# A two-layer encoder trunk on one core: the expert stage rewritten in blocks of 32 slots, with a ring of nine weight units

## The reference

```
h = layer_norm(DN_ALPHA * h + mix, ln1_g[l], ln1_b[l])
g_idx = top-1 of softmax(h @ w_rg + b_rg)           # one group of 4
e_val, e_loc = top-2 of the 4 experts of that group
combine[token, expert] = softmax(e_val) * g_val
for e in range(16):
    out += combine[:, e:e+1] * ((silu(h @ w_gate[e]) * (h @ w_up[e])) @ w_down[e])
h = layer_norm(DN_ALPHA * h + ffn, ln2_g[l], ln2_b[l])
```

## Time and profile before

| | |
|---|---|
| median of 3 runs | 1976.12 us (1970.1 to 1976.12) |
| the profiled execution's own time | 1975.3 us |
| its span | 1973.2 us, so 2.1 us lie outside the span |
| PE busy | 1681.7 us |
| DVE, ACT, POOL busy | 609.8, 509.5, 87.2 us |
| DMA | 547.06 MB, mean 277 GB/s |
| PE's granted clock, mean | 0.956 of full speed |

### The profile page before, as it was taken

How to read it: one execution, slowest core, us unless ns; L and a number is a source line. 1 busy time by engine, 2 the same in 40 slices (tenths; PEclk the granted TensorE clock), 3 DMA queues, 4 the chain that set the end, 5 groups by cost and what they waited for, 6 DMA issues and landing times.

```text
span 1973.2 us, 22680 instructions
## 1 busy us (share of the span) xinstructions
PE 1681.7 (85%) x9061; PEld 1086.5 (55%) x9062; DVE 609.8 (31%) x714; ACT 509.5 (26%) x562; POOL 87.2 (4%) x39
## 2 busy tenths in 40 slices
PE   5899999968878788787869999999688777887885
PEld 5799899854322223232468999988433222222332
DVE  7745645542000000000386464564510000000005
ACT  4343444311111111111234543432111111111120
POOL 4100000003000000000040000000030000000000
PEclk9899999989999999999979999999799999999998
DMA  8354455650999999999514544558249999999961
GB/s 289 134 170 140 147 169 181 242 226 22 426 428 425 425 427 426 425 427 400 180 64 171 175 144 141 176 191 312 93 170 426 426 426 427 425 426 428 426 290 43
DMA packets 119302, 547.06 MB, mean 277 GB/s; under 512 B 19940, under 2 KB 23240, under 8 KB 84680
## 3 DMA queue, kind: packets, MB, share of 16 engines
q1 hardware_dynamic: 117600, 546.02, 69.6%
q10 hardware_dynamic: 1640, 0.13, 0.1%
HBM read 544.04 MB, written 2.10 MB: 277 GB/s over the span
## 4 chain that ended last, share of the span: by engine, by line
PE 55%; DMA 24%; PEldq 5%; DVE 5%; issue 5%; PEld 2%; ACT 2%; DVEq 1%; SPq 0%; ACTq 0%
DMA ring<-in_w_up_dram 24%; PE ps L705 20%; PE ps L843 9%; PE ps L900 6%; PEldq L681 5%; PE ps L702 4%; PE ps L917 4%; PE ps L881 3%; PE ps L954 3%; PEld ps L900 2%; DVE w_lo L964 1%; DVE hT_lo L964 1%; PE ps L945 1%; PE ps L667 1%; DVE arena L964 1%
## 5 line engine op out<-in xcount | busy, mean ns | idle before, releaser
L900 PE MATMUL ps<-ring,arena 128*64 128x512 f32 x2048 | 482.0, 625 | 99.0 <-DMA ring<-in_w_up_dram 75.5
L900 PEld LDWEIGHTS ps<-ring,arena 128*64 128x64 f32 x2048 | 175.5, 143 | 384.9 <-issue 384.9
L964 DVE TENSOR_TENSOR w_lo<-ring,w_hi 128x2048 fp32r<-128x2048 f32 x120 | 283.9, 2378 | 260.1 <-ACT w_hi L433 259.6
L705 PE MATMUL ps<-hT_hi,w_hi 128*128 128x256 f32 x1152 | 333.4, 289 | 25.1 <-DVE w_lo L964 24.6
L705 PE MATMUL ps<-hT_hi,w_lo 128*128 128x256 f32 x1152 | 330.0, 286 | 0.0
L705 PE MATMUL ps<-hT_lo,w_hi 128*128 128x256 f32 x1152 | 329.7, 286 | 0.0
L433 ACT ACTIVATE w_hi<-ring 128x2048 fp32r<-128x2048 f32 x120 | 228.0, 1914 | 250.0 <-PE ps L705 133.4
L964 DVE TENSOR_TENSOR arena<-arena,ps 128x256 f32<-128x256 f32 (+1 forms) x34 | 15.9, 468 | 793.4 <-ACT arena L630 793.2
L705 PEld LDWEIGHTS ps<-hT_hi,w_hi 128*128 128x128 f32 x1152 | 225.3, 196 | 28.7 <-issue 17.9
L917 PE MATMUL ps<-ring,arena 128*64 128x512 f32 x1024 | 226.8, 595 | 15.1 <-ACT arena L632 15.1
L705 PEld LDWEIGHTS ps<-hT_hi,w_lo 128*128 128x128 f32 x1152 | 225.3, 196 | 0.7 <-issue 0.5
(11 more groups left out here) (216 smaller groups left out, 1346.3 us busy)
## 6 DMA issues: line engine op xcount, KB each, us to landing
ring<-in_w_down_dram SPq DMA_DIRECT2D x64, 2048.0 KB, 18.3
ring<-in_w_gate_dram SPq DMA_DIRECT2D x64, 2048.0 KB, 16.3
ring<-in_w_up_dram SPq DMA_DIRECT2D x64, 2048.0 KB, 20.7
ring<-in_w_in_dram SPq DMA_DIRECT2D x88, 1024.0 KB, 4.8
ring<-in_w_out_dram SPq DMA_DIRECT2D x32, 1024.0 KB, 5.1
ring<-in_ln_g_dram SPq DMA_DIRECT2D x3, 1024.0 KB, 5.9
ring<-in_ln_b_dram SPq DMA_DIRECT2D x3, 1024.0 KB, 6.9
h<-in_x_dram SPq DMA_DIRECT2D x2, 1024.0 KB, 6.2
```

The lines of the kernel that those rows point to most:

```text
L705: last = eng.matmul(ps[:, b + o // 2, (o % 2) * T:(o % 2) * T + T], w_[:, o * P:o * P + P], x_[:, kk, :], start=opens and o % 2 == 0, stop ...
L900: last = eng.matmul(ps[64 * c:64 * c + BLK, 0, :], xe[:, k, :], ring[:, 0:2, k * 512 + c * 256:k * 512 + c * 256 + 256], start=(k == 0), s ...
L964: return eng.tensor_tensor(o, a, b, op)
```

## The change

Blocks have 32 slots. No rows are sorted ahead: in every block PE gathers the rows of the *next* block from h (`gather`, 8 products of 512 columns in four column groups; h is now the streamed operand, and its elements are read 64 bytes apart), turns them (`turn_rows`, 4 transposes), and scatters the outputs of the block *before* (`scatter`, 8 products whose contraction is 32 slots, in four row groups and four PSUM banks). The second four of these wait for DVE to have added the first four's banks into acc (`add_block`). Gate and up take 64 products of 256 columns in four column groups, down takes 16 of 512 in four. DVE marks the next block's slots (`mark`) and builds the scatter's matrix (`place`). The gather, transposes and scatter over all slots are gone, and so are yT, xgT and ySort. h must have its gain and bias before the gather, so that `affine(gb)` moves up to right after the transposes of the router, half of its first product on DVE. The ring has nine units of 16 KB of each partition (2.1 MB) instead of six; two units are released at a time. The expert loop is written out 16 times, with a loop only for the blocks beyond an expert's last. Before that, x is loaded in four pieces, the first `normalize` no longer waits for the parameters' transpose, the softplus stands between splits 17 and 18 (slab three of the trunk), and `affine(gb_in)` waits until PE has used nine quarters.

```diff
-BLK = 64
+BLK = 32
 KB = 256
-SLOTS = 3
...
+    SLOTS = 9
+    PER_E = 6
...
+        SLOT_KIB = (64, 80, 112, 0, 16, 128, 32, 48, 96)
...
+                    eng.wait_ge(units_used, PER_E * E * l - 2)
+                for n in range(2):
                     load_quarter(l, n)
+                if l:
+                    eng.wait_ge(units_used, PER_E * E * l)
+                for n in range(2, UNITS):
+                    load_quarter(l, n)
...
+                for u in range(PER_E * E):
+                    e, i = u // PER_E, u % PER_E
+                    if u >= SLOTS:
+                        eng.wait_ge(units_used, PER_E * E * l + u - SLOTS + 1)
+                    elif u == 2:
+                        eng.wait_ge(w_used.sem, w_used.at(l, 4 * N_IN))
+                    elif u == 3:
+                        eng.wait_ge(w_used.sem, w_used.at(l, NQ - 4))
+                    elif u == 4:
+                        eng.wait_ge(w_used.sem, w_used.at(l, NQ - 2))
+                    elif u == 6:
+                        eng.wait_ge(w_used.sem, w_used.at(l, NQ))
+                    if i < 4:
+                        for m, w in enumerate((w_gate, w_up)):
+                            src = w[l, e].rearrange("(p k) n -> p k n", k=KD)
+                            eng.dma_start(unit_gu(u)[:, m], src[:, 4 * i:4 * i + 4, :]).then_inc(unit_loaded[u % SLOTS], 16)
...
+                eng.wait_ge(w_used.sem, w_used.at(l, 9))
                 affine(gb_in)
                 eng.wait_ge(gb1_loaded.sem, gb1_loaded.at(l, 32))
-                eng.wait_ge(gath_done.sem, gath_done.at(l, KD))
-                affine(gb)
+                eng.wait_ge(xnT_done, (2 * l + 2) * 8)
+                eng.tensor_tensor(h[:, 1, :], h[:, 1, :], gb[:, 0, :], ALU.mult)
+                eng.drain()
+                eng.tensor_tensor(h[:, 1, :], h[:, 1, :], gb[:, 1, :], ALU.add).then_inc(h_ready, 1)
+                eng.wait_ge(aff_mul.sem, aff_mul.at(l, 1))
+                eng.tensor_tensor(h[:, 0, :], h[:, 0, :], gb[:, 1, :], ALU.add).then_inc(h_ready, 1)
...
+                for t in range(NT):
+                    last = eng.activation(acc[:, t, :], h[:, t, :], ACT.Copy)
+                last.then_inc(acc_ready.sem, 1)
+                with eng.Fori(0, nb) as j:
+                    g = g0 + j
+                    eng.wait_ge(gu_done, g + 1)
+                    eng.activation(sgate, ps[:, 0, 0:P], ACT.Silu).then_inc(sg_ready, 1)
+                    copy_of(xrow_done, g + l + 2, xrow, 3, xrow_ready)
+                    copy_of(hmT_done, g + 1, hmT, 1, hmT_ready)
+                    copy_of(xT_done, g + l + 2, xe, 3, xe_ready)
+                    copy_of(y_done, g + 1, yraw, 2, y_ready)
...
+                def gather(count):
+                    eng.wait_ge(hot_ready, count)
                     for t in range(NT):
...
+                        for c in range(4):
+                            r0 = BLK * c
+                            last = eng.matmul(ps[r0:r0 + BLK, 3, :], hot[:, t, :],
+                                              h[:, t, :].rearrange("a (p k) -> a k p", k=KD)[:, 4 * c:4 * c + 4, :],
+                                              start=(t == 0), stop=(t == NT - 1), tile_position=(0, r0))
+                    last.then_inc(xrow_done, 1)
+                def turn_rows(count):
+                    eng.wait_ge(xrow_ready, count)
+                    for q in range(4):
+                        last = eng.transpose(ps[:, 3, q * P:q * P + P], xrow[:, q * P:q * P + P], ident[:])
+                    last.then_inc(xT_done, 1)
...
+                def scatter(g):
+                    eng.wait_ge(place_ready, g + l + 1)
+                    eng.wait_ge(y_ready, g + 1)
                     for t in range(NT):
...
+                        for c in range(4):
+                            r0 = BLK * c
+                            eng.wait_ge(added, (g + l) * 8 + 4 * t + c + 13)
+                            eng.matmul(ps[:, 4 + c, :], place[r0:r0 + BLK, t * P:t * P + P], yraw[r0:r0 + BLK, :],
+                                       start=True, stop=True, tile_position=(r0, 0)).then_inc(sc_done, 1)
...
+                    eng.wait_ge(xe_ready, g + l + 1)
+                    for i in range(4):
+                        u = PER_E * e + i
+                        loaded(u)
+                        for k in range(4):
+                            x0 = (4 * k + i) * BLK
+                            for c in range(4):
+                                r0 = BLK * c
+                                last = eng.matmul(ps[r0:r0 + BLK, 0, 0:2 * P], xe[:, x0:x0 + BLK],
+                                                  unit_gu(u)[:, :, k, c * P:c * P + P],
+                                                  start=(i == 0 and k == 0), stop=(i == 3 and k == 3), tile_position=(0, r0))
...
+                    gather(g + 2 * l + 2)
+                    scatter(g)
                     eng.wait_ge(hm_ready, g + 1)
...
+                    eng.transpose(ps[:, 1, 0:P], hmid, ident[:]).then_inc(hmT_done, 1)
+                    turn_rows(g + l + 2)
                     eng.wait_ge(hmT_ready, g + 1)
                     for f in range(KF):
+                        u = PER_E * e + 4 + f // 2
                         if f % 2 == 0:
...
+                            loaded(u)
+                        for c in range(4):
+                            r0 = BLK * c
+                            last = eng.matmul(ps[r0:r0 + BLK, 2, :], hmT[:, BLK * f:BLK * f + BLK],
+                                              unit_down(u)[:, f % 2, c * 512:c * 512 + 512],
...
+                gather(g0 + 2 * l + 1)
+                for i in range(2):
+                    for j, col in ((0, pos12), (1, wts)):
+                        for t in range(NT):
+                            last = eng.matmul(banks(4, 2)[:, (2 * j + i) * T + t * P:(2 * j + i) * T + t * P + P],
+                                              col[:, i, t, :].to_broadcast([P, P]), ident[:], start=True, stop=True)
+                last.then_inc(spread_done.sem, 1)
+                turn_rows(g0 + l + 1)
+                eng.wait_ge(spread_ready.sem, spread_ready.at(l, 1))
+                for e in range(E):
+                    n, g1 = expert_row(eng, 0, e), expert_row(eng, 1, e)
                     with eng.If(n > 1):
                         with eng.Fori(0, n - 1) as j:
...
+                            expert_block(g1 + j, e, False)
+                    expert_block(g1 + n - 1, e, True)
+                scatter(g0 + nb)
...
-                splits(15, 21)
+                splits(15, 18)
+                if l == 0:
+                    softplus()
+                splits(18, 21)
...
+                eng.wait_ge(xnT_done, (2 * l + 2) * 8)
+                tt(h[:, 0, :], h[:, 0, :], gb[:, 0, :], ALU.mult).then_inc(aff_mul.sem, 1)
...
+                def mark():
+                    for t in range(NT):
+                        ts(hot[:, t, :], block_iota, pos12[:, 0, t, :], None, ALU.is_equal)
                     eng.drain()
...
+                    for t in range(NT):
+                        last = eng.scalar_tensor_tensor(hot[:, t, :], block_iota, pos12[:, 1, t, :], hot[:, t, :],
+                                                        ALU.is_equal, ALU.add)
+                    last.then_inc(hot_ready, 1)
+                    eng.drain()
+                    ts(block_iota, block_iota, float(BLK), None, ALU.add)
+                def add_block(g):
+                    for t in range(NT):
+                        for c in range(4):
+                            eng.wait_ge(sc_done, (g + l) * 8 + 4 * t + c + 1)
+                            sl = acc[:, t, c * 512:c * 512 + 512]
+                            tt(sl, sl, ps[:, 4 + c, :], ALU.add).then_inc(added, 1)
...
+                with eng.Fori(0, nb) as j:
+                    g = g0 + j
+                    eng.wait_ge(sg_ready, g + 1)
+                    tt(hmid, sgate, ps[:, 0, P:2 * P], ALU.mult).then_inc(hm_ready, 1)
+                    add_block(g)
+                    eng.scalar_tensor_tensor(place, rows[:, 0, :], slot_col, rows[:, 2, :], ALU.is_equal, ALU.mult)
+                    eng.scalar_tensor_tensor(place_2, rows[:, 1, :], slot_col, rows[:, 3, :], ALU.is_equal, ALU.mult)
+                    eng.drain()
+                    tt(place, place, place_2, ALU.add).then_inc(place_ready, 1)
+                    ts(slot_col, slot_col, float(BLK), None, ALU.add)
+                    mark()
+                    eng.drain()
+                add_block(g0 + nb)
+                eng.drain()
                 for t in range(NT):
...
+                    for c in range(N_OUT):
+                        eng.bn_stats(stats[:, t, c, :], acc[:, t, c * 512:c * 512 + 512])
+                normalize(2 * l + 2, acc, LN_EPS / ALPHA ** 2)
```

(17 more changed lines are left out.)

447 lines of the change are left out of this document (169 added, 278 removed).

## The result

The changed kernel takes **2111.9 us** (2103.6 to 2124.1, 4 runs) where the kernel before takes 1976.1: 1.069 times as long, interval 1.061 to 1.077. The prediction was 1958 us, in a range that ended at 2020. The profiled execution took 2120.1 us with a span of 2117.6.

What follows compares the result with a forecast made beforehand. It took PE to bound the trunk and DMA the experts, with two-block experts becoming PE-bound; 1973.2 + 1.1 (expert stage) - 18.9 (trunk) = 1955.4 us span, 2.1 outside, median 0.8 above: 1958 us, range 1908 to 2020.

Steps and rivals of the forecast that it cites:

- A block of 32 slots: PE's work per block in the expert stages: gate and up, down, transposes, scatter and gather sum to 19.0 us.
- the load row: Profile row of weight loads from h at the same stride: 340 ns against 190 contiguous, implying a 4.3 us gather.
- the price of an expert: Per expert on PE beside its blocks: 1.43 us of register loads and branches plus drains, 2.2 us.
- a rival at 2021 us: Row groups not overlapping, or written-out loop's instructions late while DMA is full: +2.1 us a block; chance 0.14.
- the clock: Low clock (0.82) was counted only for the first gather, ahead of the first gate product.
- The pace: Expert stages: DMA paces layer 0's first seven experts to 174 us, then PE; stages of 523 and 502 us.
- Every microsecond of a block costs 30 us: Both expert stages: each microsecond more per block adds 17 + 13 = 30 us in total.
- The start of the stage: Router to first gate product: sorting's gather goes, POOL's affine comes in; first gate product at 462, 18.5 us earlier.
- POOL's collision: Router: POOL's affine instructions hold up DVE's small ones, so the logits' addition and its chain come about 11 us later.
- The starts of the trunk: Trunk of both layers: earlier splits save 13.8 and 11.1 us, less 3 each; sum -18.9 us.
- POOL's wait: Trunk: POOL's four affine instructions return behind quarter nine and delay DVE, +3 us in each layer.
- The rival of a gather at 4.3 us: Strided gather at its upper end: a block costs 20.8 us, total 2012 us; chance of 1982 or more 0.24.

Runs made afterwards that it cites:

- rows: The changed kernel with the gather reading 512 neighbouring features of each row, transposes and weight rows following; 2032.6 us, 1.029.
- resident: The changed kernel with four copies of a block per layer's TensorE program instead of 32, three of them in a loop; 2041.7 us, 1.033.
- skip_small: Kernel written out for this input's block counts, plus a jump over 16 products (64 instructions) ahead of each one-block expert; 2028.5 us, 1.028.
- skip_half: Kernel written out for this input's block counts, plus a jump over 64 products (256 instructions) ahead of each one-block expert; 2064.4 us, 1.046.
- early: The changed kernel with the scatter's first 128 rows moved ahead of the gather, the second 128 behind it; 1961.0 us, 0.9916.
- no_nine: The changed kernel without GpSimd's wait for the ninth quarter before its affine pass over h; 2121.4 us, 1.072.

## Why the prediction was wrong, step by step

Laid over the profile (span 2117.6 against 1955.4), the miss of 162 us stands in two places: from the first gate product to the end of the last down product, layer 0 took 600.5 us where I had 523 (+77.5), layer 1 583.6 where I had 502 (+81.6). All else together is 3 us.

- **A block of 32 slots: right at full clock.** Gate 7.11 (7.0), down 3.57 (3.55), transposes 0.70 (1.05), scatter with its wait 4.75 (4.9). Row groups overlap. Only the gather was mis-sized: 3.43 to 3.61 us where I took 2.5, some 53 us in 47 blocks (by its group, 177.5 us for 49 gathers). The upper end of 4.3, for which the load row and the Trainium skill's rule on 16-byte lines (SBUF — State Buffer, section Door 1: The DMA port swizzle) spoke, was nearer. The stride counts, but by 1.7 us a gather (3.54 against 1.85), and not by the 2.4 of the load row; why less, no run shows. I chose between the two rows by kind, not by stride. The 79 us that rows got back are more than the miss, for there the gather falls to 1.85, below my 2.5.
- **Failed: the price of an expert.** "Per expert come 1.43 us in which PE loads its registers and branches" was read from a program whose two copies of a block stood in a loop. That program, too, jumped over one of them at every expert (some 212 instructions, counted as below), and it cost no more: the jump by itself is cheap. Written out, the jump over a copy (394 instructions: the 197 passes of a block and as many weight loads) stops PE for 7 to 8.8 us in most cases. The comparison of the groups puts the excess at 157.4 - 78.0 = 79 us of issue (78.0 is resident's, on the group of gate and up of its page); against the 2.2 us for each of 32 experts in my sum it is 87. I had named the fetch as part of a rival at 2021 us, but with full queues as its cause. The 7.01 us at a DMA share of 0.01 in rows show that they are not needed, skip_small and skip_half that the distance counts. The Trainium skill (Runtime: NRT & Kernel Launch, section Instruction fetch mechanics) says that code comes in blocks of 16 KiB over the sequencer's own queue and that a jump to code not yet loaded waits for a fetch. The trace agrees: 2.38 MB in 145 packets are 16.4 KB each. PE stands for up to 8.8 us here.
- **Failed: the clock.** I costed waits inside a block at their own length, and the router's first gather alone at low clock. In the changed kernel the wait of the scatter on DVE's adds, 36.6 us in its group and in plain view in my own sum ("in which PE mostly waits"), and the idle behind the jumps took the clock to 1.2 GHz again and again: 0.83 on average over the first seven experts. Kernel early and the windows show it. The sum has no clock term. One was due: 37 us in down (by early) and some 46 in gate and up (379.9 us busy, where 47 times 7.11 are 334), for example 6.37 instead of 3.66 us for the 64 passes behind a jump.
- **The pace.** I had DMA pace the seven experts with one block, to end at 174 us, and PE the nine others, 349 more. They took 217.8 and 382.7. An expert with one block came to some 31 to 33 us on PE (32.6 from the first gate product at 487.09 to the next at 519.73) instead of 21.2, more than its weights' 29.5, so nothing covered the excess. "Every microsecond of a block costs 30 us" holds only while DMA paces the others; here rows got back 79 us for 1.7 us a block, that is all 47 blocks. With the causes taken away the seven take 175.4 us, as the sum had it. The account closes, as an estimate: 87 us of jumps, 53 of the gather and 83 of the clock are 223 beyond the 963 of PE's work in my sum (47 blocks at 19.0, 32 experts at 2.2), where the two stages measured 1184. The sum hid 62 us of PE's slack behind the weights; none was hidden, and 221 - 62 are the 159 us of the two stages.
- **The start of the stage: right.** First gate product 26.9 us earlier than before (453.6 against 480.5), 29.3 expected with the trunk's part. POOL's collision is there as worked out; DVE's timeline in the router, with rows of 3.95 and 4.38 us against 0.20 at the earlier trace rows:

```profile
422.65 3.95 DVE L960 TENSOR_TENSOR room<-room 128x8 f32<-128x8 f32 x1
426.68 4.38 DVE L960 TENSOR_TENSOR room<-room,desc 128x8 f32<-128x8 f32 x1
```

- **The starts of the trunk: right in layer 0.** The last output product starts 10.5 us earlier (10.8 expected); POOL's wait costs 1 us there by no_nine, not 3. In layer 1, from the aggregate (1066.0) to the first gate product (1504.8) are 438.8 us, 437.2 expected.
- **The rival of a gather at 4.3 us** (2012 us; the first in the prediction's list, though its text calls it the second) had the right sign and part of the cause. None of the rivals had the size, since each was taken alone and at full clock; the range ended at the worse of two of them, and here three causes came together.

## What to carry to other kernels

Price a written-out copy of code by what is jumped over: on TensorE a jump over 64 instructions took 1.2 to 1.5 us, one over 394 some 8 in most cases, and a loop that holds its copies brought the fetches back from 145 packets to 55. Where PE waits on another engine inside a short block, put independent products into the wait before anything else: here it bought the wait and the clock behind it. And check whether a stage has cover at all before costing an excess at a part of it.

## What was not expected of the hardware

- The code that is jumped over seems to be fetched all the same: 145 packets with 17 blocks skipped, 115 without them, and 120 and 133 with 64 and 256 instructions skipped 17 times.
- A long idle behind a jump does not need full DMA queues: 7.01 us at a share of 0.01, beside 8.64 at 0.82 and 7.88 at 1.01.
- The same wait of some 0.7 us on DVE inside the scatter is followed by a down product at full clock in 24 blocks and by a slower one in 23.
- Four column groups that stream 512 elements 64 bytes apart: 16 passes take 3.54 us, and 1.85 where the elements are neighbours. For weight loads the same stride took 298 ns instead of 190.
- What stays open: what part of the 8 us is the fetch itself and what goes on around it. In seven idles looked at, of three kernels, the one packet of the instruction queue moved 4.3 to 5.9 us after PE stopped, and PE went on 2.7 to 2.8 us after it; no run took either part further.
